# Expert layers' last combination: sums of squares three tiles behind the products, weight splits behind tiles 5 and 7

## What is computed

```
y = jnp.einsum('becf,efd->becd', hid, w_down) * gate[..., None]
x = x + g2 * jnp.zeros_like(h).at[bidx, idx].add(y)
...
def rms_norm(x, g):
    xf = x.astype(jnp.float32)
    y = xf * lax.rsqrt(jnp.mean(xf * xf, axis=-1, keepdims=True) + EPS)
    return (y * g.astype(jnp.float32)).astype(x.dtype)
```

## Time and profile before

| | us |
|---|---|
| median of 3 runs | 1434.03 (1432.86 to 1434.76) |
| the profiled execution | 1432.99 |
| its span | 1431.2 |
| PE busy in it | 1194.1 (83%) |
| DVE busy | 624.0 (44%) |
| ACT busy | 432.4 (30%) |
| POOL busy | 78.2 (5%) |
| mean granted TensorE clock | 0.935 of full |

### The profile page before, as it was taken

The page is one execution under the profiler, slowest core; times in us unless marked ns, Lnnn a source line. Parts: engine busy times, 40 slices in busy tenths (PEclk is TensorE's granted clock), DMA queues, the critical chain, the costliest instruction groups (busy, mean ns, idle before and its releaser), DMA issues.

```text
span 1431.2 us, 19546 instructions
## 1 busy us (share of the span) xinstructions
PE 1194.1 (83%) x8265; PEld 887.2 (62%) x8265; DVE 624.0 (44%) x1136; ACT 432.4 (30%) x777; POOL 78.2 (5%) x118
## 2 busy tenths in 40 slices
PE   5899898998986556669999655666999999999887
PEld 3677567785852113139986211313899878899756
DVE  3645775646430001136653000112995456545574
ACT  2436333322310000034331000002554554443562
POOL 3000123540000000000000000000000000000000
PEclk9999899999989889889999988988999979999898
DMA  9845844426589999994549999999245303444000
GB/s 327 293 154 176 295 166 164 141 68 239 208 341 409 409 409 409 409 341 152 194 181 364 410 409 409 409 409 354 68 170 176 118 1 130 165 177 174 5 1 30
DMA packets 125099, 338.65 MB, mean 237 GB/s; under 512 B 8657, under 2 KB 11590, under 8 KB 125014
## 3 DMA queue, kind: packets, MB, share of 16 engines
q1 hardware_dynamic: 117536, 334.51, 61.6%
q10 hardware_dynamic: 7478, 2.91, 0.8%
HBM read 336.35 MB, written 1.05 MB: 236 GB/s over the span
## 4 chain that ended last, share of the span: by engine, by line
PE 59%; DMA 25%; DVE 10%; ACT 3%; issue 1%; ACTq 1%; SPq 1%; DVEq 0%
PE bank L685 9%; PE bank L687 9%; PE bank L686 9%; DMA expert_slots<-in_w_up_dram 7%; DMA weight_ring<-in_w_down_dram 6%; DMA arena<-in_w_gate_dram 4%; DMA arena<-in_w_up_dram 3%; DVE arena L1879 3%; PE bank L974 3%; DMA weight_ring<-in_w_gate_dram 3%; PE bank L592 2%; PE bank L1140 2%; PE bank L550 2%; PE bank L812 2%; PE bank L664 1%
## 5 line engine op out<-in xcount | busy, mean ns | idle before, releaser
L685 PE MATMUL bank<-input_high,weights_high 128*128 128x256 f32 (+1 forms) x992 | 290.8, 293 | 7.5 <-DVE input_low L1879 7.5
L686 PE MATMUL bank<-input_low,weights_high 128*128 128x256 f32 (+1 forms) x992 | 284.0, 286 | 0.0
L687 PE MATMUL bank<-input_high,weights_low 128*128 128x256 f32 (+1 forms) x992 | 283.9, 286 | 0.0
L1879 DVE TENSOR_TENSOR weights_low<-weight_ring,weights_high 128x1024 fp32r<-128x1024 f32 x144 | 176.1, 1224 | 182.4 <-ACT weights_high L1435 182.0
L685 PEld LDWEIGHTS bank<-input_high,weights_high 128*128 128x128 f32 x992 | 188.6, 190 | 12.8 <-issue 9.9
L1435 ACT ACTIVATE weights_high<-weight_ring 128x1024 fp32r<-128x1024 f32 x144 | 151.7, 1055 | 143.4 <-PE bank L687 143.1
L686 PEld LDWEIGHTS bank<-input_low,weights_high 128*128 128x128 f32 x992 | 188.2, 190 | 0.8
L687 PEld LDWEIGHTS bank<-input_high,weights_low 128*128 128x128 f32 x992 | 188.7, 190 | 0.0
L1879 DVE TENSOR_TENSOR arena<-arena,bank 128x512 f32<-128x512 f32 (+1 forms) x38 | 24.8, 652 | 275.8 <-PE bank L974 245.8
L974 PE MATMUL bank<-weight_ring,arena 128*32 128x512 f32 x480 | 68.5, 705 | 48.0 <-DMA weight_ring<-in_w_up_dram 25.9
L974 PEld LDWEIGHTS bank<-weight_ring,arena 128*32 128x32 f32 x480 | 15.9, 120 | 96.3 <-issue 39.9
(11 more groups left out here) (410 smaller groups left out, 1722.4 us busy)
## 6 DMA issues: line engine op xcount, KB each, us to landing
weight_ring<-in_ada_w_dram SPq DMA_DIRECT2D x24, 2048.0 KB, 8.9
weight_ring<-in_w_gate_dram SPq DMA_DIRECT2D x20, 2048.0 KB, 21.2
weight_ring<-in_w_down_dram SPq DMA_DIRECT2D x16, 2048.0 KB, 23.7
arena<-in_w_up_dram SPq DMA_DIRECT2D x12, 2048.0 KB, 24.2
arena<-in_w_down_dram SPq DMA_DIRECT2D x12, 2048.0 KB, 23.8
expert_slots<-in_w_up_dram SPq DMA_DIRECT2D x10, 2048.0 KB, 24.7
weight_ring<-in_w_up_dram SPq DMA_DIRECT2D x10, 2048.0 KB, 23.8
weight_ring<-in_even_w_in_dram SPq DMA_DIRECT2D x9, 2048.0 KB, 8.2
```

Of the source, the lines that this page charges most:

```text
L685: pe.matmul(b[:, 0:width], hi[:, k, :], XHI[:, k, t0:t0 + width], start=k == 0, stop=False)
L686: pe.matmul(b[:, 0:width], hi[:, k, :], XLO[:, k, t0:t0 + width], start=False, stop=False)
L687: mm = pe.matmul(b[:, 0:width], lo[:, k, :], XHI[:, k, t0:t0 + width], start=False, stop=k == KD - 1)
L1879: return dve.tensor_tensor(out_, a, b, op)
```

## The change

`norm_behind` gets a distance `lag`, by default 1 as before. The two last combinations of the expert layers give it 3: `norm_part` for tile m - 3 stands behind the product for tile m, and after tile 7 those of tiles 4, 5, 6 and 7 follow. ACT's two `high()` move from behind tiles 3 and 4 to behind tiles 2 and 5, DVE's two `split()` from behind tiles 3 and 4 to behind tiles 5 and 7. No instruction is added or removed.

```
-            def norm_behind(i, width, sq):
+            def norm_behind(i, width, sq, lag=1):
 
                 def after(m):
-                    if m >= 1:
-                        norm_part(i, m - 1, width, sq)
+                    if m >= lag:
+                        norm_part(i, m - lag, width, sq)
                     if m == KD - 1:
-                        norm_part(i, m, width, sq)
+                        for k in range(KD - lag, KD):
+                            norm_part(i, k, width, sq)
                 return after
...
-                combine((GROUPS - 1,), "combine", norm_behind(2 + 2 * ly, T, SQn))
+                combine((GROUPS - 1,), "combine", norm_behind(2 + 2 * ly, T, SQn, 3))
...
-                    if names[0] != "combine" or m in (3, 4):
+                    if names[0] != "combine" or m in (2, 5):
                         high()
...
                 for m in range(KD):
                     residual(ly, 40, m)
-                    if m in (3, 4):
+                    if m in (5, 7):
                         split()
```

## The result

The change makes the kernel faster. In the first comparison its median is 1415.48 us (4 runs, 1413.28 to 1421.59) beside 1433.53 us, a ratio of 0.9879 with a 95% interval of 0.9855 to 0.9903. By that ratio it is 17.3 us less (the medians lie 18.05 us apart); the forecast was 13.2 us less and 1420.8 us, with a range that began at 1416.5. The profiled execution has a span of 1414.2 us.

The account below looks back on a forecast made before the run. The bound was taken to move between stages, with waits among engines in the two last combinations; 7.8 + 5.4 = 13.2 us less than the 1431.2 us span, plus 1.0 for the median, gave 1420.8 us, range 1416.5 to 1427.5.

Parts of the forecast that it names:

- The ring of waits: Layer 0's last combination: PE's sum waits for square, residual, split, high part; PE stands 1.92 us twice, the split 1.43.
- Layer 0, 7.8 us: Layer 0's last combination: the logarithm starts at 629.4 instead of 637.20, 7.8 us less, assuming the full clock.
- The walk: Layer 0's last combination stepped through with profiled durations; only some 0.3 us idle, before sum 6, in 7.4 us.
- Layer 1, 5.4 us between 4.6 and 6.3: Layer 1's last combination: 4.6 us less if half clock lasts to 990.1, 6.3 if until 986.7; the middle taken.
- the lower branch: Layer 1's last combination: the half clock stays until 990.1 as before, giving 4.6 us less.
- The landing at the start of the high part: Layer 0: the first high part's weight chunk lands at 624.5, its start is 624.55; slack 0 to 0.1 us.
- What is won lasts to the end: Behind both combinations: dense products and layer 1's experts start earlier by the whole amount.
- rival 3: Tail behind the last L897: two more sums in layer 0, four units in layer 1; slower, 1436.6 to 1439.2; chance 0.03.
- rival 2: Both combinations: the ring is only moved, not broken; 1 us or less gained, 1433 us; chance 0.05.
- rival 1: One of the two combinations wins little; 1427.4 or 1426.2 us; chance 0.15.
- The size of the gain, 13.2 us: Both last combinations together: 7.8 us in layer 0 plus 5.4 in layer 1.
- The sum: Whole kernel: profiled span 1431.2 less 13.2 is 1419.8; with the median 1.0 above the profiled execution, 1420.8 us.

Follow-up runs that it names:

- high parts early: The change with ACT's high parts behind tiles 0 and 3 instead of 2 and 5; ratio 0.9925 to the kernel before, layer 0's combination 8.88 us.
- squares first: The change, with ACT squaring layer 1's meta tokens ahead of the logarithm's table load; ratios 0.9879 and 0.9868 to the kernel before, mean 1412.1 us.
- both together: The change with squares first and two warming products ahead of layer 1's meta-token sums; ratio 0.9913 to the kernel before, mean 1418.8 us.
- layer 1 alone: The kernel before with the whole change in layer 1's last combination only; ratio 0.9956, mean 6.6 us less, combination 11.77 us.
- layer 0 alone: The kernel before with the whole change in layer 0's last combination only; ratio 0.9943, mean 7.7 us less, combination 7.48 us.

## Why the prediction was right and wrong

- *The ring of waits and what breaks it*: right. The two waits of 1.43 us are gone, and of the waits for squares 0.36 us are left. Taken alone, each half of the change brings a part (3.4 and 5.0 us in layer 0).
- *Layer 0, 7.8 us*: right, 7.77 us. The walk's 0.3 us of idle time before sum 6 are there too, as 0.36 us before its weight load.
- *Layer 1, 5.4 us between 4.6 and 6.3*: right, 5.03 us against the first profile and 6.1 against the second. PE was the bound in the change's profiles, 13.1 us with 5.1 us at half clock; with the clock full all through it took 11.8, of which 0.9 are a wait for the first square. Which clock comes did stay open. The trace took the lower branch, in which the half clock lasts as before: 6.83 us both times. It began 1.77 us ahead of the first product and not 0.77, so it covered 1.0 us less of the combination, worth 0.5 us at PE's half speed; that is what lies between 4.6 and 5.03. The rule of the Trainium skill (TensorE: Matmul & The Clock Gate, Part 1), that activity releases the throttled clock, was to bring it back sooner in the filled stretch. The three profiles of the change don't show that: PE was busy in all of 969.93 to 976.76 and the clock stayed at half. In high parts early, squares first (twice) and both together it was back after 3.4 us, as the rule would have it; why they differ is open.
- *The landing at the start of the high part*: right. It was as close as the rows had said, and two tiles earlier the high part waits 0.97 us for it.
- *What is won lasts to the end*: right; both layers alone show it (7.7 and 6.6 us by the means).
- *The tail of two more sums as a loss (rival 3), no change (rival 2), half of it (rival 1)*: none came.
- *The size of the gain, 13.2 us*: it holds against all runs, 14.2 us with an interval of 11.7 to 16.7, or 15.3 (12.9 to 17.7) against those made beside it. The interval of the first comparison alone, 13.9 to 20.8 us, leaves it just outside.
- *From the size to a time*: this is the step that failed. The sum took the profiled 1432.99 and left all but the two combinations as it stood there; in the change's profile the rest took 4.2 us less (5.76 less ahead of the change, 1.56 more behind layer 0's combination), and the second profile of the unedited kernel is 4.9 us shorter ahead of it as well. Then comes its last step, "The median of the runs stands 1.0 above the profiled one, so the median would be 1420.8", and with it the range's "1 either side for the spread of the runs before". Three runs of the kernel before, all near 1434, were taken for its level; 85 runs have a mean of 1430.6 and a standard deviation of 4.1. With that level the forecast would have been 1417.4, beside the 1416.4 of the change's 16 runs. That the changed kernel's first four runs came out 1.9 us below 1417.4 is within the scatter of four runs with a standard deviation of 4.7. The range rested on the same three runs, so it was too narrow by the scatter of such a median, some 2.5 us either way as one standard error (an estimate from the standard deviations). For the same reason the 0.2% that the prediction held to be tellable from no change is too little: the kernel before against itself has an interval of 0.9966 to 1.0017. That a shift may move the times at half clock elsewhere was written down, but priced at 1.5 us, where the last stage alone differs by 4.4 us between two profiles of the unedited kernel and by 10 over all.

## What to carry to other kernels

Where engines pass tiles around a ring (product, residual, square, sum) and one of them has an in-order queue, put enough products ahead of the first consumer that the queue never waits for its own result, and put side work that needs another engine's result where that result is already old. Time the ring first: if a turn is longer than PE's work per tile, both the order on PE and the side work on the others are on the path, and each brings a part.

And before an absolute time is forecast, look at how far one kernel's executions lie apart: three that agree within 2 us may come from a spread of 20.

## What the runs showed of the hardware

The same instructions took quite different times from one execution to the next. In the last stage they went with the clock. Behind layer 1's combination all these kernels are the same, 2904 products of PE in each profile. That whole stage as one stretch (us, PE busy, clock, DMA share, GB/s), first of layer 1 alone, then of the change, then of layer 0 alone:

```profile
996.85:1420.40 423.55, 400.78 (x2904) 0.97 0.30 105
```
```profile
984.83:1414.20 429.37, 407.28 (x2904) 0.95 0.29 102
```
```profile
987.81:1421.50 433.69, 411.47 (x2904) 0.94 0.28 100
```

The lower the clock, the longer the stage, and PE's busy time moves with it. By the clock records of the 14 traces the stage has 27.8 us at half clock where it takes 423.55; 34.9 with 425.60 and 425.61; 44.9 to 45.3 with 429.1 to 429.5; 51.8 and 51.9 with 432.00 and 431.84; 55.4 to 55.8 with 433.5 to 433.7. Much of it lies in one place, the scan of the recurrent layer. There, in the kernel before, then in layer 1 alone:

```profile
1140.00:1150.00 10.00, 8.78 (x75) 1.00 0.00 0
1150.00:1160.00 10.00, 10.00 (x70) 0.69 0.01 2
1160.00:1170.00 10.00, 10.00 (x47) 0.50 0.00 0
```
```profile
1135.00:1145.00 10.00, 8.78 (x74) 1.00 0.02 6
1145.00:1155.00 10.00, 10.00 (x90) 1.00 0.01 2
1155.00:1165.00 10.00, 9.37 (x60) 0.83 0.01 2
```

PE has work without a gap and still drops to half clock, in one execution for 17.1 us and in the other for 3.4. The same 146 products (the stage's 1047th to 1193rd) take 24.8 us in the first and 19.8 in the second. Many of them load few columns of weights (L1103 64, L1092 16). Why one execution falls there for longer than another was not settled; that such differences come without the change is shown by the unedited kernel, 429.11 and 433.48 us in two profiles.

The stage ahead of layer 0's combination, 615.4 to 622.0 us, is another matter, and it stays open. There the time doesn't follow the clock: the unedited kernel's slower profile (621.96) has 78.5 us at half clock, its faster one (617.04) 85.3. They part early: product 150 of PE starts at 45.01 us in the slower and at 43.38 in the faster, though the clock was full up to there in the slower one; product 300 at 74.29 and 71.17, product 1200 at 234.28 and 229.02.
